# Cached-value rounds and gate quarters moved to other steps of the delta rule in a one-core hybrid decoder step

## The chip, the core and the metric

The program runs on one core of a Trainium2 chip. TensorE (PE) multiplies, VectorE (DVE) and ScalarE (ACT) read its results out of PSUM, GpSimd (POOL) helps with elementwise work, and SyncE (SP) issues most of the transfers. The metric is the device time of one execution in microseconds (us), the median of the runs.

## What is computed

One decoder layer for a prompt of 512 tokens and for 8 sample tokens with cached keys and values of 2048 positions each. One projection of the normalised input feeds two mixers and two gates; cut to what matters here:

```python
qkv, z, b_lg, a_lg, qb, kb, vb, ga, gb = in_proj(hp, norm1_w, w_in)     # ga, gb: 2 x 1024 gate columns
# A: gated delta rule, chunk by chunk (here chunks of 128 tokens, 4 chunks)
t_inv = triangular_solve(a + eye, eye)                                  # per chunk and head
v_new = ui - wi @ state
o = (qi * exp(gi)) @ state + qki @ v_new
state = state * exp(g_last) + k'^T @ v_new
y_a = (rmsnorm(o) * silu(z)) @ w_proj_a
# B, sample tokens: attention over the cached pages chosen by q . mean(k)
o = softmax(logits) @ cached values
y_b = o @ w_proj_b
mixed = sigmoid(ga) * y_a + sigmoid(gb) * y_b
```

After it come the output projection, the MLP and a final norm. The outputs are the activations, the new keys and values, and the new states.

## The kernel before

All matmuls are float32. A large one is split in three (high x high, high x low, low x high), in `product` at L463. A "unit" is 128 output columns of a weight for all 520 tokens: ScalarE makes the high half of the weights (`split_high`, L447), VectorE the low half (`split_low`, L452). The 16 gate units, two sets of 8, are each cut into quarters of 12 matmuls; `gate(n, first, last)` issues them, and a unit's last quarter is followed on ScalarE by its tanh (L1037), then by the high half for the unit two further on.

The order is written out by hand. `delta_order()` lists 92 steps: the stages of the delta rule for chunk 0, then 2 (slot 0) interleaved with those of chunk 1, then 3 (slot 1), four stages behind. `delta_fill()` hangs other work on each step by its number: gate quarters, low halves (`low`), rounds of cached values (`round`), the mask after each fourth round (`mask`). Each engine walks the same list, does its part of the stage, then its part of the step's fills, `low` first.

The stages of a chunk: sums, decays, turn, products, start; then left and right of levels 1 to 6 of the triangular inverse (left: four transposes L2222 and small products L2168 or L2228, each copied out by ScalarE; right: small products L2168 or L2239, taken over by VectorE with a mask, L1620, or a copy, L1622); inverse_k, new_v, new_state (products for the state, then for the output o, all L2155); normalise (ScalarE squares o at L1111, VectorE reduces it, ScalarE takes the root at L1114); turn_out (VectorE scales by the root's reciprocal, L1585 and L1586, and PE turns the result, L2175); keep_out.

A **round** (`value_round`, L2146) multiplies weights of one sample token with four pages of cached values, in two halves of two pages. The pages lie in `ring`, which holds four halves: so pages of a round are asked for only once the round two before it has been done. SP issues these loads (L601). Each sample token takes 4 rounds, 32 in all; the first round of a token also waits until VectorE has read the last token's result out of the bank (`keep_values`, L1573 and L1576). In the version before, rounds 0 to 25 and gate units 1 to 8 are hung on the steps, and units 9 to 15 come behind the last step with rounds 26 to 31 between whole units.

The lines of the delta loop that place this work on PE:

```python
for what, k in filled[i]:
    if what == "gate":
        gate(k // 4, 2 * (k % 4), 2 * (k % 4) + 2)
    ...
    elif what == "round":
        value_round(k)
```

Of the kernel before, what the change touches and what calls it, by code (L numbers as in the profile page):

```python
# [26 lines left out]
ALU = mybir.AluOpType  # L27
ACT = mybir.ActivationFunctionType
# [6 lines left out]
P = 128  # L35
# [87 lines left out]


KEYS_BEFORE = sum(keys_in_unit(u) for u in range(U_C)) + sum(keys_in_step(n) for n in range(NA))
ROUNDS_DELTA = 26
GATES_DELTA = 9


def delta_fill():  # L130

    fill = [[] for _ in range(len(delta_order()))]
    for i in range(GROUPS - KEYS_BEFORE):
        fill[i - (i >= 9)].append(("key", i))
    quarters = [0, 1, 1, 2, 2, 3, 3, 6, 8, 9, 10, 11, 13, 14, 16, 17, 18, 19, 20, 21, 36, 42, 43, 45, 46, 47, 48, 82, 83, 88, 89]
    for i, at in enumerate(quarters):
        fill[at].append(("gate", 5 + i))
    for name, at in (("sm_prep", 2), ("sm_bcast", 4), ("sm_bc", 4), ("sm_turn", 8), ("sm_delta", 9), ("sm_osq", 10), ("sm_osum", 12),
                     ("sm_oms", 13), ("sel_turn", 15), ("sel_red", 16), ("sel2_turn", 17), ("select", 18), ("bias", 20),
                     ("lg_bias", 21), ("lg_exp", 21), ("row_sums", 22), ("den", 25), ("den_out", 26), ("sm_oroot", 36), ("sm_on", 39),  # L140
                     ("sm_oh", 40), ("sm_onl", 41)):
        fill[at].append((name, 0))
    for u, at in ((3, 3), (4, 6), (5, 14), (6, 19), (7, 30), (8, 47), (9, 60)):
        fill[at].insert(0, ("low", u))
    for half in range(2):
        fill[5 + half].append(("sm_kv", half))
        fill[6 + half].append(("sm_rows", half))
    for k in range(3):
        fill[11 + k].append(("tail", k))
        fill[12 + k].append(("tail_out", k))  # L150
    for r in range(ROUNDS_DELTA):
        at = 24 + 13 * r // 5 + (r == 24)
        fill[at].append(("round", r))
        if r % 4 == 3:
            fill[at + 1].append(("mask", r // 4))
            if r == 15:
                fill[at + 2].append(("turn_values", 0))
    return fill
# [43 lines left out]
def hybrid_step(nc, const_f, const_m, x_prompt, x_sample, cache_k, cache_v, page_table, state_delta, state_conv,  # L202
# [9 lines left out]
    with ExitStack() as ctx:  # L212
# [123 lines left out]
        sts7 = at("sts7", [P, HA, DA], F32, ht_at + 3 * NT * 4)  # L336
        sqc = at("sqc", [P, 2 * HA, DA], F32, d0 + 16384)
        gate_b = at("gate_b", [P, 8, NT], F32, d0)
        mh = at("mh", [P, KT, NT], F32R, r1)
        ml = at("ml", [P, KT, NT], F32R, r1 + 16640)  # L340
        sga = at("sga", [P, NT], F32, r1 + 53248)
# [14 lines left out]
        def unit_ps(b):  # L356

            return ps[:, b * 1024 + 256:b * 1024 + 256 + NT]
# [130 lines left out]
            return unit_ps(u % 2 if u else 3)  # L489

        def gate_ps(n):
            return unit_ps(0 if 0 < n < GATES_DELTA else 1 if n == 0 else n % 2)

        def slot_banks(p):

# [322 lines left out]
        def _(act):  # L818
# [210 lines left out]
            def gate(n):  # L1029

                u = U_GATE + n
                if n < 12:
                    load_unit(act, u + 4)
                act.wait_ge(unit_done, u + 1)
                if n == 3:
                    act.wait_ge(*done("sm_kv1"))
                A((gate_a if n < 8 else gate_b)[:, n % 8], gate_ps(n), ACT.Tanh, scale=0.5).then_inc(S["gate_out"], 1)  # L1037
                split_high(act, u + 2)

            gate(0)  # L1040
# [109 lines left out]
            act.wait_ge(S["s_out"], NCH)  # L1150
            act.dma_start(sd_prompt[0, 0].rearrange("h d e -> d h e"), st[:, NCH % 2]).then_inc(stored, 16)
            act.wait_ge(S["ona_l_out"], NCH)
            for n in range(9, 15):
                gate(n)
            act.wait_ge(*done("os_ready"))
            A(onb_h[:, :, SEQ:NT], s4[:, 0:32].rearrange("p (c b) -> p c b", c=4), ACT.Copy).then_inc(*did("os_h"))
# [67 lines left out]
        def _(v):  # L1224
# [364 lines left out]
            for i, (stage, c) in enumerate(delta_order()):  # L1589
# [89 lines left out]
                        keep_values(n)  # L1679
                if i == 0:  # L1680
                    split_low(v, U_GATE + 2)
            split_low(v, U_GATE + 10)
            split_low(v, U_GATE + 11)
            keep_values(6)
            for u in range(U_GATE + 12, U_GATE + 17):
                split_low(v, u)
            keep_values(7)
            v.wait_ge(S["vb_turned"], 2)
# [19 lines left out]
            for j in range(8):  # L1708
                u = U_MERGE + j
                v.wait_ge(unit_done, u + 1)  # L1710
                v.wait_ge(S["gate_out"], 16)
                b = 2 * (1 - j % 2)
                link(STT(sga[:], gate_a[:, j], 1.0, unit_ps(b), ALU.add, ALU.mult))
                link(STT(sgb[:], gate_b[:, j], 1.0, unit_ps(b + 1), ALU.add, ALU.mult))
                if j >= 1:
                    v.wait_ge(S["mh_out"], j)
                TT(mx_[:], sga[:], sgb[:], ALU.add).then_inc(S["mix_ready"], 1)
                if j < 7:
                    split_low(v, u + 2)
                v.wait_ge(S["mix_ready"], j + 1)  # L1720
                v.wait_ge(S["mh_out"], j + 1)
                STT(ml[:, j], mx_[:], 0.5, mh[:, j].bitcast(F32), ALU.mult, ALU.subtract).then_inc(S["ml_out"], 1)
                v.wait_ge(S["ml_out"], j + 1)
# [86 lines left out]
        def _(pe):  # L1810
# [478 lines left out]


            pe.wait_ge(S["on_gated"], NCH - 1)
            gate(9)
            value_round(26)
            gate(10)
            value_round(27)
            gate(11)
            value_round(28)
            gate(12)
            value_round(29)
            gate(13)  # L2300
            value_round(30)
            gate(14)
            value_round(31)
            gate(15, 0, 4)
            turn_values(1)
# [108 lines left out]
```

## Time and profile before

| | before |
|---|---|
| median of 3 runs (lowest to highest) | 967.5 us (966.75 to 967.82) |
| the profiled execution: its time | 968.5 us |
| its span, first to last instruction | 966.0 us |
| PE busy | 936.7 us, 97% |
| DVE, ACT, POOL busy | 516.3, 400.9, 231.4 us |
| mean granted TensorE clock | 0.992 of 2.4 GHz |
| first round to last round | 329.3 to 483.9 us |

The profiled execution took 2.5 us more than its span, and 1.0 us more than the median of the runs. PE is busy nearly throughout, so what can change is where PE stands idle, and busy time of a merged row in which PE waited between matmuls.

### The profile page before, as it was taken

What the parts mean: (1) busy time and instruction counts of PE and PEld (TensorE: products, weight loads), DVE (VectorE), ACT (ScalarE), POOL (GpSimd) and SP (SyncE); (2) the same over time, 40 slices, a digit from 0 to 9 for tenths busy, and PEclk for the clock granted to TensorE, in tenths of its full rate; (3) what the DMA queues carried; (4) which work ended last, traced back from release to release, by engine and by line L of the source; (5) the groups of instructions that cost most, each with busy time, mean ns of one, the idle gap of its engine ahead of it and who ended that gap; (6) DMA issues with size and microseconds to landing.
All of it is one profiled execution on the core that took longest, in us unless ns stands there. A gap on an engine that the chain in (4) does not pass through costs nothing.

```text
span 966.0 us, 21253 instructions
## 1 busy us (share of the span) xinstructions
PE 936.7 (97%) x8658; PEld 879.7 (91%) x8658; DVE 516.3 (53%) x718; ACT 400.9 (41%) x695; POOL 231.4 (24%) x137
## 2 busy tenths in 40 slices
PE   5999999999997999999999999999999999999997
PEld 5999999999986776568899999999999999999997
DVE  6227598887886633433156556753344344334444
ACT  7435555556753345323122343521352144224433
POOL 0005975667779003000000002661000000000000
PEclk8999999999998999999999999999999999999999
DMA  8546696776686387877724852323322233344312
GB/s 252 171 169 220 211 304 194 216 217 194 187 270 209 96 255 239 278 238 239 219 69 125 271 152 87 89 88 98 100 88 88 88 92 101 89 139 122 89 41 88
DMA packets 184173, 156.50 MB, mean 162 GB/s; under 512 B 9217, under 2 KB 146123, under 8 KB 183702
## 3 DMA queue, kind: packets, MB, share of 16 engines
q1 hardware_dynamic: 165126, 141.33, 48.0%
q10 hardware_dynamic: 18968, 14.07, 4.8%
q8 instruction: 56, 0.92, 0.4%
q14 instruction: 23, 0.19, 0.1%
HBM read 146.51 MB, written 8.95 MB: 161 GB/s over the span
## 4 chain that ended last, share of the span: by engine, by line
PE 84%; POOL 4%; DVE 4%; issue 3%; DMA 2%; ACT 1%; SPq 1%; DVEq 0%; ACTq 0%; POOLq 0%
PE ps L463 69%; PE ps L2146 3%; POOL ring L769 3%; PE ps L2155 3%; PE ps L1998 2%; PE ps L1816 1%; DMA ring<-in_cache_v 1%; PE ps L1965 1%; PE ps L2168 1%; PE ps L1855 1%; PE ps L1988 1%; PE ps L2175 1%; DVE w_low L452 1%; DMA w_raw<-in_w_in 1%; PE ps L2222 1%
## 5 line engine op out<-in xcount | busy, mean ns | idle before, releaser
L463 PE MATMUL ps<-xh,w_high 128*128 128x256 f32 x1216 | 256.4, 292 | 1.4 <-DVE w_low L452 0.9
L463 PE MATMUL ps<-xl,w_high 128*128 128x256 f32 x1216 | 245.3, 283 | 0.0
L463 PE MATMUL ps<-xh,w_low 128*128 128x256 f32 x1216 | 245.3, 283 | 0.0
L452 DVE TENSOR_TENSOR w_low<-w_raw,w_high 128x1024 fp32r<-128x1024 f32 x125 | 163.8, 1311 | 150.9 <-ACT w_high L447 150.6
L447 ACT ACTIVATE w_high<-w_raw 128x1024 fp32r<-128x1024 f32 x125 | 132.2, 1058 | 262.3 <-PE ps L463 258.7
L463 PEld LDWEIGHTS ps<-xh,w_high 128*128 128x128 f32 x1216 | 187.8, 189 | 16.3 <-issue 11.4
L463 PEld LDWEIGHTS ps<-xh,w_low 128*128 128x128 f32 x1216 | 189.1, 189 | 0.0
L463 PEld LDWEIGHTS ps<-xl,w_high 128*128 128x128 f32 x1216 | 188.9, 189 | 0.0
L769 POOL TENSOR_TENSOR ring<-ring,qb 128x1024 f32<-128x1024 f32 x64 | 152.9, 2411 | 130.9 <-DVE mtqk L1287 74.4
L463 PE MATMUL ps<-ml,w_high 128*128 128x256 f32 (+1 forms) x640 | 128.9, 283 | 0.0
L463 PE MATMUL ps<-mh,w_low 128*128 128x256 f32 (+1 forms) x640 | 128.9, 283 | 0.0
L463 PE MATMUL ps<-mh,w_high 128*128 128x256 f32 (+1 forms) x640 | 128.5, 282 | 0.0
L463 PEld LDWEIGHTS ps<-ml,w_high 128*128 128x128 f32 x640 | 99.2, 188 | 0.0
L463 PEld LDWEIGHTS ps<-mh,w_low 128*128 128x128 f32 x640 | 99.2, 188 | 0.0
L463 PEld LDWEIGHTS ps<-mh,w_high 128*128 128x128 f32 x640 | 99.2, 188 | 0.0
L1272 DVE TENSOR_REDUCE lg<-ring 128x16 f32<-128x1024 f32 x64 | 77.3, 1214 | 17.2 <-POOL ring L769 17.1
L1763 DVE TENSOR_TENSOR ht<-ps,ht 128x520 f32<-128x520 f32 x31 | 21.7, 700 | 90.8 <-PE ps L463 90.8
L809 POOL TENSOR_TENSOR state<-state,sbc 128x512 f32<-128x512 f32 x8 | 10.9, 1367 | 227.3 <-PE ps L463 227.3
L2146 PE MATMUL ps<-ring,lg 128*32 128x512 f32 x256 | 42.2, 619 | 0.7 <-DMA ring<-in_cache_v 0.6
L1181 ACT ACTIVATE mh<-uu 128x520 fp32r<-128x520 f32 x32 | 20.5, 639 | 38.2 <-DVE uu L1768 38.2
L1752 DVE TENSOR_TENSOR ml<-uu,mh 128x520 fp32r<-128x520 f32 x32 | 22.4, 701 | 24.8 <-ACT mh L1181 24.8
L953 ACT ACTIVATE prob<-ps,nbias 128x128 f32<-128x128 f32 (+3 forms) x32 | 16.8, 525 | 28.0 <-DVE nbias L1385 28.0
(375 smaller groups left out, 1116.8 us busy)
## 6 DMA issues: line engine op xcount, KB each, us to landing
ring<-in_cache_k SPq DMA_DIRECT2D x128, 256.0 KB, 3.3
ring<-in_cache_v SPq DMA_DIRECT2D x128, 256.0 KB, 3.5
w_raw<-in_w_in SPq DMA_DIRECT2D x66, 256.0 KB, 3.9
w_raw<-in_w_up SPq DMA_DIRECT2D x64, 256.0 KB, 3.1
w_raw<-in_w_down SPq DMA_DIRECT2D x64, 256.0 KB, 3.0
w_raw<-in_w_in ACTq DMA_DIRECT2D x24, 256.0 KB, 4.2
w_raw<-in_w_out SPq DMA_DIRECT2D x16, 256.0 KB, 3.2
ht_dram<-ht ACTq DMA_DIRECT2D x1, 2080.0 KB, 15.3
```

Of the source, the lines that this page charges most:

```text
L447: act.activation(w_high[:, u % 2], w_raw[:, s], ACT.Copy).then_inc(S_hi, 1)
L452: dve.tensor_tensor(w_low[:, u % 2], w_raw[:, u % 4], w_high[:, u % 2].bitcast(F32), ALU.subtract).then_inc(S_lo, 1)
L463: last = pe.matmul(out[:, a:b], w[:, u % 2, k, :], x[:, i, a:b], start=(first + i == 0 and w is w_high and x is rhs_h), stop=(first + i == ...
L769: g.tensor_tensor(ring[:, r % 4], ring[:, r % 4], bc(qb[:, b:b + 1, :], [P, 2, WB]), ALU.mult)\
L953: A(prob[:, n % 2, 0:N], score_bank(n, N), ACT.Exp, scale=-1.0, bias=nbias[:, n % 3:n % 3 + 1], accum_out=rs[:, n:n + 1]).then_inc(S["att_ ...
L1181: A(mh[:, i - 1], uu[:, (i - 1) % 2], ACT.Copy).then_inc(S["uh_out"], 1)
L1272: v.tensor_reduce(lg[:, b, :, 2 * r:2 * r + 2].rearrange("p h g -> p g h"), ring[:, i % 4].rearrange("p g (h d) -> p g h d", d=DB), AX.X, ...
L1752: TT(ml[:, i - 1], uu[:, (i - 1) % 2], mh[:, i - 1].bitcast(F32), ALU.subtract)\
L1763: TT(ht[:, j], unit_ps((U_MLP + i) % 2), ht[:, j], ALU.add).then_inc(S["h_out"], 1)
L1998: last = mm(rows_bank[:, h * DB:(h + 1) * DB], probt[:, n % 2, t * P:(t + 1) * P], mtv[:, t, h * DB:(h + 1) * DB], start=(t == 0), stop=(t ...
L2146: last = mm(bank(6)[32 * strip:32 * strip + 32, :], lg[:, b].rearrange("p h (s r) -> p r (h s)", r=4)[:, part], ring[:, g % 4, i, :], star ...
L2155: last = mm(out[:, h * P:(h + 1) * P], left(h), right(h), start=(i == 0), stop=(i == len(pairs) - 1), skip_group_check=True)
```

## The change

It replaces the formula that spaced the rounds by a list of steps, hangs 24 rounds in place of 26 on the steps, and leaves eight for the end, where they stand between parts of the last gate units. The quarters of gate units 6 to 8 move to other steps, and unit 9 joins them, in ten-unit numbering (`GATES_DELTA = 10`). So that gate units 8 and 9 can be kept while the delta rule still uses its buffers, their results go to a new place, `gate_89`, in memory that the chunks 0 and 1 of `tm` have left. The low halves 7 to 10 move with them.

```diff
-ROUNDS_DELTA = 26
-GATES_DELTA = 9
+ROUND_ITEMS = (24, 27, 29, 31, 33, 38, 40, 42, 45, 48, 50, 54, 56, 58, 62, 66, 69, 72, 75, 78, 80, 81, 84, 87)
+GATES_DELTA = 10
...
-    for r in range(ROUNDS_DELTA):
-        at = 24 + 13 * r // 5 + (r == 24)
+    for r, at in enumerate(ROUND_ITEMS):
...
+        gate_89 = at("gate_89", [P, 2, NT], F32, r1 + 33280)
...
-            return unit_ps(0 if 0 < n < GATES_DELTA else 1 if n == 0 else n % 2)
+            return unit_ps(0 if 0 < n < GATES_DELTA else 1 if n == 0 else (n + 1) % 2)
...
-                A((gate_a if n < 8 else gate_b)[:, n % 8], gate_ps(n), ACT.Tanh, scale=0.5).then_inc(S["gate_out"], 1)
+                A(kept_gate(n), gate_ps(n), ACT.Tanh, scale=0.5).then_inc(S["gate_out"], 1)
...
-            gate(9)
+            value_round(24)
+            gate(10, 0, 6)
+            value_round(25)
+            gate(10, 6, 8)
+            gate(11, 0, 4)
             value_round(26)
-            gate(10)
+            gate(11, 4, 8)
+            gate(12, 0, 2)
             value_round(27)
-            gate(11)
+            gate(12, 2, 8)
             value_round(28)
-            gate(12)
+            gate(13, 0, 4)
             value_round(29)
-            gate(13)
+            gate(13, 4, 8)
+            gate(14, 0, 2)
             value_round(30)
-            gate(14)
+            gate(14, 2, 8)
             value_round(31)
```

Behind the step at which gate unit 5 ends, the quarters of units 6 to 8 stood at steps 21, 36, 42, 43, 45, 46, 47, 48, 82, 83, 88 and 89, and stand at 21, 28, 30, 32, 39, 41, 47, 50, 55, 58, 62 and 68; unit 9 has 72, 75, 81 and 84. The low halves 7, 8, 9 stood at 30, 47, 60 and stand at 29, 43, 57; the tenth is new at 74.

Below, numbers behind names (`sqb_128`) are buffers; line numbers from L1037 on are 3 higher in the changed kernel.

**The end of the delta rule, PE.** L2155 (L2158) is new_state of chunk 3, L463 a gate unit, L2175 (L2178) the transposes of turn_out of chunk 3, L2146 (L2149) a round. Before:

```order
L2155 MATMUL ps<-st,qgt 128x128
L2155 MATMUL ps<-An,qkt 128x128
L2155 MATMUL ps<-st,qgt 128x128
L2155 MATMUL ps<-An,qkt 128x128
L463 MATMUL ps<-xh,w_high 128x256
L463 MATMUL ps<-xh,w_high 128x264
```

Of the change:

```order
L2158 MATMUL ps<-An,qkt 128x128
L2158 MATMUL ps<-st,qgt 128x128
L2158 MATMUL ps<-An,qkt 128x128
L2178 MATMUL ps<-cf,sqb_128 128x128 x4
L2149 MATMUL ps<-ring,lg 32x512 x4
L463 MATMUL ps<-xh,w_high 128x256
```

Two gate quarters and a round stood between new_state and turn_out of chunk 3; now nothing does. ScalarE at the same place, from the copies of chunk 2's last products on (L1114 or L1117 the root, L1037 or L1040 the tanh of a gate). Before:

```order
L1103 ACTIVATE Dm<-ps 128x512
L1119 ACTIVATE ona_h<-An 128x4x128
L1106 ACTIVATE An<-ps 128x512
L1111 ACTIVATE sqb_128<-ps 128x512
L1114 ACTIVATE on_st<-on_st 128x4
L437 DMA w_raw<-in_w_in 128x4x128 x2
L1037 ACT_TABLE_LOAD
```

Of the change:

```order
L1040 ACT_TABLE_LOAD
L1040 ACTIVATE gate_154<-ps 128x520
L447 ACTIVATE w_high<-w_raw 128x1024
L1106 ACTIVATE Dm<-ps 128x512
L1122 ACTIVATE ona_h<-An 128x4x128
L1109 ACTIVATE An<-ps 128x512
L1114 ACTIVATE sqb_128<-ps 128x512
L1117 ACT_TABLE_LOAD
L1117 ACTIVATE on_st<-on_st 128x4
```

A tanh of gate unit 9 now stands ahead, so the root of chunk 3 has a table load of its own; over the program ScalarE has two rows more, both of them such loads.

**The first turn_out, PE.** From the output products of chunk 0 (L2155, L2158) over left and right of level 6 of chunk 1 to turn_out of chunk 0 (L2175, L2178). Before, with the first two rows of a gate quarter's twelve:

```order
L2155 MATMUL ps<-An,qkt 128x128 x4
L2146 MATMUL ps<-ring,lg 32x512 x4
L2222 MATMUL ps<-cf,Em 64x64 x4
L2228 MATMUL ps<-Em,An 64x64 x4
L463 MATMUL ps<-xh,w_high 128x256
L463 MATMUL ps<-xh,w_high 128x264
```

Of the change:

```order
L2158 MATMUL ps<-An,qkt 128x128 x4
L2225 MATMUL ps<-cf,Em 64x64 x4
L2231 MATMUL ps<-Em,An 64x64 x4
L2242 MATMUL ps<-sqb_128,Dm 64x64 x4
L2178 MATMUL ps<-cf,sqb_127 128x128 x4
L2149 MATMUL ps<-ring,lg 32x512 x4
```

Two rounds and a quarter have gone from between the output products and turn_out.

**The mask at step 43, VectorE.** L1632 (L1635) is the state of chunk 1, L1576 (L1579) the mask that round 8 waits for, L452 a low half. Before:

```order
L1486 TENSOR_TENSOR ona_l<-sn,ona_h 128x4x8
L1632 SCALAR_TENSOR_TENSOR st<-st,glx,ps 128x128 x4
L1576 SCALAR_TENSOR_TENSOR vb<-ps,cf,vb 128x512
L1598 TENSOR_TENSOR sqb_127<-tm,egc 128x512
L1637 TENSOR_REDUCE on_st<-sqb_128 128x4
```

Of the change:

```order
L1489 TENSOR_TENSOR ona_l<-sn,ona_h 128x4x8
L1635 SCALAR_TENSOR_TENSOR st<-st,glx,ps 128x128 x4
L452 TENSOR_TENSOR w_low<-w_raw,w_high 128x1024
L1579 SCALAR_TENSOR_TENSOR vb<-ps,cf,vb 128x512
L1601 TENSOR_TENSOR sqb_127<-tm,egc 128x512
```

The low half of gate unit 8 has moved ahead of the mask.

## Rows read from the trace of the kernel before

**Rows 1.** The page, busy us (share of the span) and instructions by engine

```profile
PE 936.7 (97%) x8658; PEld 879.7 (91%) x8658; DVE 516.3 (53%) x718; ACT 400.9 (41%) x695; POOL 231.4 (24%) x137
```

**Rows 2.** Windows: us, PE, PEld, DVE, ACT, POOL busy, clock, DMA share, GB/s

```profile
295.00:300.00 5.00, 1.89 (x42) 1.22 (x42) 4.79 (x15) 1.25 (x3) 5.00 (x3) 0.94 0.71 231
300.00:305.00 5.00, 3.33 (x16) 3.34 (x17) 5.00 (x5) 1.67 (x3) 5.00 (x4) 0.50 0.42 127
```

**Rows 3.** Tile view of the value ring, 326 to 490 us

```profile
L2146 PE MATMUL ps<-ring,lg x256: 592/619/650, 329.3 to 483.9; 128*32 128x512 f32 x128
...
  DMA ring<-in_cache_v: 6.8, 11
...
DMA to landing us min/median/max: 2.6/3.5/6.2
```

**Rows 4.** Timeline of PE: start us, us, line, tiles; four rounds

```profile
335.83 1.95 PE L2146 MATMUL ps<-ring,lg 128*32 128x512 f32 x8
...
405.70 2.23 PE L2146 MATMUL ps<-ring,lg 128*32 128x512 f32 x8
...
410.17 2.12 PE L2146 MATMUL ps<-ring,lg 128*32 128x512 f32 x8
...
414.49 1.10 PE L2146 MATMUL ps<-ring,lg 128*32 128x512 f32 x8
```

**Rows 5.** Waits of PE, 329 to 500 us: total us, times, longest

```profile
PE ps L2168 <- ACT qgt L1088: 0.7, 1, 0.7
PE ps L2168 <- ACT sqb L1098: 0.6, 2, 0.4
...
PE ps L2222 <- DVE Em L1620: 0.6, 1, 0.6
PE ps L2175 <- ACT An L1055: 0.5, 1, 0.5
...
PE ps L2175 <- DVE Dm L1611: 0.2, 1, 0.2
```

**Rows 6.** Timelines of PE, ACT and DVE up to turn_out of chunk 0

```profile
347.31 0.50 PE L463 MATMUL ps<-xh,w_high 128*128 128x256 f32 x2
...
348.94 0.68 PE L2239 MATMUL ps<-sqb,Dm 64*64 64x64 f32 x8
...
347.41 0.38 ACT L1100 ACTIVATE sqb<-ps 64x256 f32<-64x256 f32 x1 [0.23 <-PE ps L2228]
347.81 1.28 ACT L1114 ACT_TABLE_LOAD   x1
...
349.55 0.69 DVE L1586 TENSOR_TENSOR sqb<-ps,on_st 128x512 f32<-128x512 f32 x1
```

**Rows 7.** Timelines of PE, ACT and DVE up to turn_out of chunk 3

```profile
438.02 0.48 PE L463 MATMUL ps<-xh,w_high 128*128 128x256 f32 x2
...
442.11 0.66 PE L2175 MATMUL ps<-cf,sqb 128*128 128x128 f32 x4
...
438.30 0.60 ACT L1111 ACTIVATE sqb<-ps 128x512 f32<-128x512 f32 x1 [3.31 <-PE ps L2155]
439.86 0.20 ACT L1114 ACTIVATE on_st<-on_st 128x4 f32<-128x4 f32 x1 [0.96 <-DVE on_st L1638]
...
440.31 0.69 DVE L1586 TENSOR_TENSOR sqb<-ps,on_st 128x512 f32<-128x512 f32 x1
```

**Rows 8.** Timelines of DVE and PE around the state of chunk 1

```profile
336.61 1.21 DVE L452 TENSOR_TENSOR w_low<-w_raw,w_high 128x1024 fp32r<-128x1024 f32 x1
...
360.37 1.12 DVE L1632 SCALAR_TENSOR_TENSOR st<-st,glx,ps 128x128 f32<-128x128 f32 x4 [5.23 <-PE ps L2155]
361.41 0.74 DVE L1576 SCALAR_TENSOR_TENSOR vb<-ps,cf,vb 128x512 f32<-128x512 f32 x1
...
361.88 0.49 PE L463 MATMUL ps<-xh,w_high 128*128 128x256 f32 x2
```

**Rows 9.** Timeline of ACT, the high half behind a gate's tanh

```profile
376.22 1.05 ACT L447 ACTIVATE w_high<-w_raw 128x1024 fp32r<-128x1024 f32 x1
```

More of the change, by code:

```diff
@@ L134, in delta_fill @@
         fill[i - (i >= 9)].append(("key", i))
-    quarters = [0, 1, 1, 2, 2, 3, 3, 6, 8, 9, 10, 11, 13, 14, 16, 17, 18, 19, 20, 21, 36, 42, 43, 45, 46, 47, 48, 82, 83, 88, 89]
+    quarters = [0, 1, 1, 2, 2, 3, 3, 6, 8, 9, 10, 11, 13, 14, 16, 17, 18, 19, 20, 21, 28, 30, 32, 39, 41, 47, 50, 55, 58, 62, 68, 72, 75, 81, 84]
     for i, at in enumerate(quarters):
@@ L142, in delta_fill @@
         fill[at].append((name, 0))
-    for u, at in ((3, 3), (4, 6), (5, 14), (6, 19), (7, 30), (8, 47), (9, 60)):
+    for u, at in ((3, 3), (4, 6), (5, 14), (6, 19), (7, 29), (8, 43), (9, 57), (10, 74)):
         fill[at].insert(0, ("low", u))
@@ L491, in gate_ps, with kept_gate @@
         def gate_ps(n):
-            return unit_ps(0 if 0 < n < GATES_DELTA else 1 if n == 0 else n % 2)
+            return unit_ps(0 if 0 < n < GATES_DELTA else 1 if n == 0 else (n + 1) % 2)
+        def kept_gate(n):
+            return gate_a[:, n] if n < 8 else gate_89[:, n - 8] if n < 10 else gate_b[:, n - 8]
         def slot_banks(p):
@@ L1152, in _ @@
             act.wait_ge(S["ona_l_out"], NCH)
-            for n in range(9, 15):
+            for n in range(10, 15):
                 gate(n)
@@ L1681, in _ @@
                     split_low(v, U_GATE + 2)
-            split_low(v, U_GATE + 10)
             split_low(v, U_GATE + 11)
+            split_low(v, U_GATE + 12)
             keep_values(6)
-            for u in range(U_GATE + 12, U_GATE + 17):
+            for u in range(U_GATE + 13, U_GATE + 17):
                 split_low(v, u)
@@ L1713, in _ @@
                 link(STT(sga[:], gate_a[:, j], 1.0, unit_ps(b), ALU.add, ALU.mult))
-                link(STT(sgb[:], gate_b[:, j], 1.0, unit_ps(b + 1), ALU.add, ALU.mult))
+                link(STT(sgb[:], kept_gate(8 + j), 1.0, unit_ps(b + 1), ALU.add, ALU.mult))
                 if j >= 1:
```

## The prediction

> **What bounds the kernel now.** First the page: PE is busy 97% of the span, no other engine much over half [rows 1]. So a change of order can only give or take time in which PE stands still, or in which a merged row of PE holds waits between its matmuls. The number of matmuls, halves, rounds and transfers is the same in both kernels, and nothing ahead of step 24 moves; I therefore look from the first round at 329.3 us on [rows 3].
>
> Second, the view of the ring: PE stood idle 6.8 us in 11 waits for pages of cached values, and a page took 2.6 to 6.2 us from its issue to its landing, median 3.5 [rows 3]. The timeline shows what such a wait costs a round. A round that finds all pages takes 1.10 us, as at 414.49; those at 335.83, 405.70 and 410.17 take 1.95, 2.23 and 2.12 [rows 4]. Ten rounds between 335.83 and 410.17 are longer than 1.10. Their excess, with 0.4 us that PE waited ahead of one of them, sums to 7.8 us. That is 1.0 more than the idle rows say, because a second half that comes late no longer overlaps the first. So 7.8 us is the most that better spacing can give.
>
> Third, the other waits of PE in this stretch: 0.7, 0.6 (two together), 0.6, 0.5 and 0.2 us, each for a copy by ScalarE or VectorE that the next product of the delta rule needs [rows 5]. They are small because gate quarters and rounds stand between a product and the one that needs it. This is the cover that the change moves.
>
> **The ring: gained.** Pages of a round are asked for when the round two before is done. In the trace the rounds that waited began 6.2 to 8.3 us after the round two before; the one at 414.49, 8.8 us after that at 405.70, did not wait [rows 4]. I added up PE's work between rounds in the new order, with each item's size from the trace (round 1.1, gate quarter 1.5 to 1.6, a left step 0.4 to 1.0, a right step 0.4 to 0.6, new_state 2 to 2.8). With the new waits below, a round now begins 7.3 to 12.9 us after the round two before; only rounds 2, 11, 12, 21 and 22 are at 8.3 or less. If these five lose a quarter of a us each, 1.2 us stays, against 0.8 for each of the ten before. Bounds: nothing stays, or 3 us does. Gain 7.8 - 1.2 = **6.6 us**, between 4.8 and 7.8.
>
> **The last turn_out (chunk 3): lost.** Before, PE's next work behind the output products began at 438.02, two gate quarters and a round, and turn_out followed at 442.11. Meanwhile ScalarE squared the output (438.30), took the root (439.86) and VectorE scaled it until 440.31 + 0.69 = 441.00 [rows 7]. So PE needed 441.00 - 438.02 = 3.0 us of other work and had 4.1. In the new order nothing stands there. The tanh of unit 9 is now ahead, so a table load of 1.28 us [rows 6] comes between square and root: 438.90 + 1.28 = 440.18 in place of 439.86, 0.3 more. PE stands still **3.3 us**, between 3.0 and 3.4.
>
> **The first turn_out (chunk 0): lost.** Two rounds and a quarter leave this place. In the trace the products of level 6 ended at 347.31, and ScalarE's copy of them at 347.41 + 0.38 = 347.79; the right step needs that copy, so without the quarter PE waits 0.5 us [rows 6]. From the copy on, table load, root, reciprocal and scaling took until 349.55 + 0.69 = 350.24, which is 2.45 us; PE has only the right step to do, 0.6 us of its row's 0.68 before the next can start [rows 6]. That leaves 1.85 us, in all **2.3 us**. Least 1.5, if ScalarE gets to the copy earlier; most 2.6.
>
> **Round 8: lost.** It starts the third token's bank and so waits for the mask, and at step 43 the low half of unit 8 now stands ahead of it on VectorE. From 361.41 the low half takes 1.21 (as at 336.61) and the mask 0.74, less 0.1 of overlap: 363.3 us. PE's output products ended at 361.88, and round 8 comes next where a quarter used to be [rows 8]. **1.4 us**, between 1.2 and 1.6. Behind the low half and the mask stand VectorE's reduction and scaling for turn_out of chunk 1; PE has a round and a turn for cover, 2.1 us, against six short operations of 2.6 us in sum: **0.4 us**, between 0 and 1.0.
>
> **Steps 50 to 54: lost.** Between products and start of chunk 2 stood a gate quarter, and PE still waited 0.2 us [rows 5]: the chain takes 1.8 us. Now a round of 1.1 stands there: **0.6 us** more. The tanh of unit 7 moves from step 48 to 50, behind the copies of start: the waits of 0.7 and 0.5 us for qgt and An [rows 5] go, but its table load, 0.6 us of tanh and 1.05 us of high half [rows 9] now stand ahead of the copy of left1. PE has a round, sums and left1 meanwhile. I take **0.9 us**, between 0 and 1.3.
>
> **Pairs of small steps: lost and gained.** Three places now have a left or right step directly ahead of the one that needs its copy, with only a small step between: right3 of chunk 2 (step 62), left6 (72) and right4 of chunk 3 (75). The rows of this kind are 0.4 and 0.6 us [rows 5]; I take 0.5 each, **1.5 us**, between 0.9 and 2.0. In return the three such waits of the kernel before (0.6 in two, 0.6) are covered, which with qgt and An makes 2.4 us gained.
>
> **At no cost.** The place of `gate_89`, the other PSUM bank of the last units and the seam between rounds and gate parts at the end: rounds there already stood among gates unhurt, and none of the last eight waited for pages. Two table loads more on ScalarE are 2.6 us of an engine that is 41% busy [rows 1]; one is in the 3.3 us above, the other lies under a gate's matmuls, and would cost its 1.28 us if that cover were gone. VectorE reads each mask in time for rounds 4, 12, 16, 20, 24 and 28, with at least 0.5 us to spare by the same durations.
>
> **The sum.** New waits 3.3 + 2.3 + 1.4 + 0.4 + 0.6 + 0.9 + 1.5 = 10.4; gone 2.4; ring gained 6.6. Net 10.4 - 2.4 - 6.6 = **1.4 us longer**. On the profiled execution that is 968.5 + 1.4 = 969.9 us; this one stood 1.0 over the median of its runs, so the median should be 967.5 + 1.4 = **968.9 us**. With the gains and losses at their ends the net runs from -3 to +5 us.
>
> **A rule on the table loads.** In the rows the load at 347.81 takes 1.28 us, and root and reciprocal are over when the scaling starts 1.74 us later [rows 6]; load, root and reciprocal alone come to 1.7, so nothing else stands between. The Trainium skill, page "ScalarE: Activation LUTs", section "What ACT_TABLE_LOAD costs", gives about 2.66 us for each switch of set, the load and a drain of 1.38 us behind it. By that the new load ahead of the last root would cost PE an estimated 1.4 us more, and the sum would be 2.8 us longer instead of 1.4. The trace leaves no room for the drain, so my sum goes by the trace.
>
> **Rivals.**
> 1. Faster: ScalarE and VectorE run ahead more than I think, because PE no longer bunches rounds. Then only the wait at the last turn_out has full size, which has nothing to stand under, and the six others shrink to the 0.5 us of the small rows [rows 5], 3.0 in all. Net 6.3 - 2.4 - 6.6 = -2.7: 964.8 us. It decides once the new waits together are under 7.1 us. For it: before, nine in ten of these steps had no wait. Against it: the chains are counted from starts and ends in the trace, and the order has nothing to put under them. Chance 0.22.
> 2. Slower, the clock: around 295 to 305 us PE was busy 1.89 and 3.33 of 5 us and the granted clock fell to 0.94 and 0.50 of 2.4 GHz [rows 2], that is to 1.2 GHz for a while, 0.3 + 2.5 = 2.8 us of full clock lost. If the stillness at the first or last turn_out does the same, 1.4 + 2.8 = 4.2: 971.7 us. Against it: there PE stood still for over half of the first stretch, here it works fully up to the last turn_out and again behind it. The Trainium skill, page "TensorE: Matmul & The Clock Gate", section "What's actually happening", has a monitor that halves the clock after idleness and restores it after steady work; the trace agrees in kind. Chance 0.1.
> 3. Slower, the spacing doesn't do it: landing takes up to 6.2 us [rows 3] and loads of units 12 and 13 now fall among the pages. If half of the 7.8 us stays, the net is 10.4 - 2.4 - 3.9 = 4.1: 971.6 us. It decides from a remainder of 1.7 us on. Chance 0.15.
> 4. Slower with the same waits, each near its upper end, 970 to 971 us: chance 0.11.
>
> **How the numbers follow.** About 0.2%, 1.9 us, is what a measurement of this kernel can tell from no change. The forecast, within 1.9 us of 967.5, has 0.42; rival 1 gives faster 0.22; rivals 2 to 4 give slower 0.36. The range reaches to rival 1's value and a little past those of 2 and 3: 964.8 to 972.3 us.
>
> **What would show it.** Right: the ring's idle under 2 us and no round over 1.9; PE idle over 3 us ahead of the last turn_out and some 2 ahead of the first, 1.4 ahead of the ninth round, for VectorE's mask. Wrong: turn_out of chunk 3 starting under 2.5 us after the last output product, a clock under 1.00 anywhere from 350 us on, or waits for `in_cache_v` over 3 us.

## The result: slower than forecast, by lost clock

| kernel | executions | median us | lowest to highest | ratio to before, 95% interval |
| --- | --- | --- | --- | --- |
| before | 4 | 967.66 | 966.75 to 968.65 | |
| changed | 4 | 974.38 | 970.16 to 977.35 | 1.0066 [1.0041, 1.0090] |
| changed, taken again (e1) | 6 | 974.79 | 972.87 to 979.61 | 1.0076 [1.0052, 1.0100] |

The forecast was 968.9 us with a range to 972.3. The kernel is 6.7 us slower. Its four executions spread over 7 us where the four of the kernel before lay within 2; the later sets of the kernel before, 19 to 22 executions each, spread over 5 to 7 us as well. One execution of the kernel before, in the set beside e9 and e10, took 4782.69 us; it is in that set's median of 968.16 us, and in no ratio, interval or mean.

The execution that was profiled is the fastest of the changed kernel, 970.16 us with a span of 967.8 us; that of before had 966.0 us. The page and PE's waits, to be read beside [rows 1] and [rows 5]:

```profile
span 967.8 us, 21255 instructions
PE 933.4 (96%) x8658; PEld 878.0 (91%) x8658; DVE 518.7 (54%) x718; ACT 403.3 (42%) x697; POOL 231.5 (24%) x137
...
PE ps L2178 <- DVE sqb L1589: 5.6, 3, 3.1
PE ps L2171 <- ACT sqb L1101: 2.0, 4, 1.0
PE ps L2149 <- DVE vb L1579: 1.2, 1, 1.2
PE ps L2158 <- ACT Dm L1106: 0.7, 1, 0.7
PE ps L2178 <- DVE Dm L1614: 0.6, 1, 0.6
PE ps L2242 <- ACT sqb L1103: 0.5, 1, 0.5
PE ps L2225 <- DVE Em L1623: 0.4, 1, 0.4
PE ps L2149 <- DMA ring<-in_cache_v: 0.4, 1, 0.4
```

Each row is who waited for whom, total us, times, longest. The first row is turn_out of chunks 3, 0 and 1. From 325 to 500 us all rows but the ring's, with one of 0.2 us that is not shown, make 11.2 us; in the same stretch of the kernel before they made 4.0.

The ring's own view, beside [rows 3]: idle before its loads and matmuls, and landing.

```profile
  DMA ring<-in_cache_v: 1.8, 2
...
DMA to landing us min/median/max: 2.4/3.3/5.6
```

The idle on pages fell from 6.8 us in 11 waits to 1.8 in 2. This view adds up the idle of weight loads and of matmuls (6.2 in 9 and 0.6 in 2 before, 1.3 and 0.4 now), so the two that are left are one late page, of round 22. Now PE around the two places with the longest waits (start us, us, line, tiles, idle before and its releaser), which are those of [rows 6] and [rows 7]:

```profile
347.07 0.68 PE L2242 MATMUL ps<-sqb,Dm 64*64 64x64 f32 x8 [0.47 <-ACT sqb L1103]
349.52 0.66 PE L2178 MATMUL ps<-cf,sqb 128*128 128x128 f32 x4 [1.78 <-DVE sqb L1589]
350.11 1.57 PE L2149 MATMUL ps<-ring,lg 128*32 128x512 f32 x8
...
445.64 0.66 PE L2178 MATMUL ps<-cf,sqb 128*128 128x128 f32 x4 [3.15 <-DVE sqb L1589]
446.23 1.94 PE L2149 MATMUL ps<-ring,lg 128*32 128x512 f32 x8
...
448.70 0.64 PE L463 MATMUL ps<-xl,w_high 128*128 128x256 f32 x2
...
449.83 0.40 PE L463 MATMUL ps<-xl,w_high 128*128 128x256 f32 x2
```

The waits are those forecast. What was not forecast stands in the rows behind them: the round after each takes 1.57 and 1.94 us where a full round takes 1.10, and no page was late for it. A pair of gate matmuls takes 0.64 us and, a microsecond later, 0.40. The windows (us; PE, PEld, DVE, ACT, POOL busy; granted clock; DMA share; GB/s) say why:

```profile
345.00:350.00 5.00, 2.75 (x30) 2.21 (x29) 2.75 (x7) 2.84 (x6) 0.00 (x0) 1.00 0.85 301
350.00:355.00 5.00, 5.00 (x29) 3.61 (x28) 1.67 (x8) 1.26 (x3) 0.00 (x0) 0.66 0.43 121
440.00:445.00 5.00, 2.50 (x23) 2.31 (x21) 2.92 (x9) 2.08 (x3) 0.00 (x0) 1.00 0.62 210
445.00:450.00 5.00, 4.36 (x22) 2.54 (x23) 3.54 (x7) 0.73 (x2) 0.00 (x0) 0.66 0.25 69
```

PE stands still for 2.3 us in two waits (0.47 and 1.78, with 0.68 of small matmuls between) and for 3.2 us in one. Right behind each, the granted clock averages 0.66 of 2.4 GHz over five microseconds. A mean of 0.66 is 3.4 us at 1.2 GHz and the rest at 2.4, and costs 0.34 x 5 = 1.7 us, twice. In the execution profiled in e1 the second is twice as long, this time over two windows:

```profile
445.00:450.00 5.00, 2.56 (x23) 2.37 (x22) 2.86 (x9) 2.08 (x3) 0.00 (x0) 0.98 0.65 210
450.00:455.00 5.00, 4.29 (x18) 2.31 (x19) 3.10 (x7) 0.63 (x1) 0.00 (x0) 0.50 0.20 56
455.00:460.00 5.00, 5.00 (x40) 4.56 (x38) 0.51 (x1) 1.28 (x1) 0.00 (x0) 0.83 0.96 295
```

There (0.02 + 0.50 + 0.17) x 5 = 3.4 us of clock go, the first part of it while PE still waits.

### The profile page after: what moved, and what is told of

Read it like the earlier page. It is cut to its first block, busy times and chain, and to the rows that moved or that the text cites. A ratio compares the mean times of both kernels' runs of the same rounds, so it can differ in the third digit from the quotient of the medians.

```text
span 967.8 us, 21255 instructions
## 1 busy us (share of the span) xinstructions
PE 933.4 (96%) x8658; PEld 878.0 (91%) x8658; DVE 518.7 (54%) x718; ACT 403.3 (42%) x697; POOL 231.5 (24%) x137
## 4 chain that ended last, share of the span: by engine, by line
PE 87%; DVE 5%; ACT 3%; DMA 1%; POOL 1%; issue 1%; SPq 0%; DVEq 0%; ACTq 0%
PE ps L463 71%; PE ps L2149 3%; PE ps L2158 2%; PE ps L2001 2%; PE ps L1819 2%; PE ps L2171 1%; POOL ring L772 1%; PE ps L1968 1%; DVE w_low L452 1%; PE ps L1991 1%; PE ps L2225 1%; DVE lg L1275 1%; PE ps L1858 1%; DMA ring<-in_cache_v 1%; PE ps L2178 0%
## 5 line engine op out<-in xcount | busy, mean ns | idle before, releaser
L463 PE MATMUL ps<-xh,w_high 128*128 128x256 f32 x1216 | 257.2, 293 | 1.4 <-DVE w_low L452 1.0
L463 PE MATMUL ps<-xl,w_high 128*128 128x256 f32 x1216 | 245.2, 283 | 0.0
L463 PE MATMUL ps<-xh,w_low 128*128 128x256 f32 x1216 | 245.0, 283 | 0.0
L452 DVE TENSOR_TENSOR w_low<-w_raw,w_high 128x1024 fp32r<-128x1024 f32 x125 | 163.4, 1308 | 148.8 <-ACT w_high L447 148.5
L463 PEld LDWEIGHTS ps<-xh,w_high 128*128 128x128 f32 x1216 | 187.8, 189 | 17.4 <-issue 12.3
L463 PEld LDWEIGHTS ps<-xl,w_high 128*128 128x128 f32 x1216 | 188.8, 188 | 0.0
L463 PEld LDWEIGHTS ps<-xh,w_low 128*128 128x128 f32 x1216 | 188.8, 189 | 0.0
L463 PE MATMUL ps<-ml,w_high 128*128 128x256 f32 (+1 forms) x640 | 128.9, 283 | 0.0
L463 PE MATMUL ps<-mh,w_low 128*128 128x256 f32 (+1 forms) x640 | 128.9, 283 | 0.0
L463 PE MATMUL ps<-mh,w_high 128*128 128x256 f32 (+1 forms) x640 | 128.5, 282 | 0.0
L463 PEld LDWEIGHTS ps<-ml,w_high 128*128 128x128 f32 x640 | 99.2, 188 | 0.0
L463 PEld LDWEIGHTS ps<-mh,w_low 128*128 128x128 f32 x640 | 99.2, 188 | 0.0
L463 PEld LDWEIGHTS ps<-mh,w_high 128*128 128x128 f32 x640 | 99.2, 188 | 0.0
L2149 PE MATMUL ps<-ring,lg 128*32 128x512 f32 x256 | 37.4, 641 | 1.7 <-DVE vb L1579 1.2
L1623 DVE COPY_PREDICATED Em<-cm,ps 128x512 f32<-128x512 uint8 x20 | 14.6, 734 | 30.6 <-PE ps L2171 30.6
```

Source lines behind the costliest of these rows:

```text
L452: dve.tensor_tensor(w_low[:, u % 2], w_raw[:, u % 4], w_high[:, u % 2].bitcast(F32), ALU.subtract).then_inc(S_lo, 1)
L463: last = pe.matmul(out[:, a:b], w[:, u % 2, k, :], x[:, i, a:b], start=(first + i == 0 and w is w_high and x is rhs_h), stop=(first + i == ...
L2149: last = mm(bank(6)[32 * strip:32 * strip + 32, :], lg[:, b].rearrange("p h (s r) -> p r (h s)", r=4)[:, part], ring[:, g % 4, i, :], star ...
```

## Work and clock, told apart

Every execution lists its span and its mean granted clock. Span times clock is about the span at full clock; span less that product is what lower clock took (a low clock while PE waits anyway is counted too, so this is an upper value). As each clock is given to three digits, a single product is good to half a microsecond; these are means over the executions.

| kernel | executions | median us | mean span | mean clock | product | lost to clock |
| --- | --- | --- | --- | --- | --- | --- |
| before | 22 | 967.57 | 965.0 | 0.9923 | 957.5 | 7.5 |
| changed, both sets | 10 | 974.4, 974.8 | 972.3 | 0.9870 | 959.6 | 12.7 |
| e2, stand-ins at both turn_outs | 8 | 971.39 | 968.9 | 0.9918 | 960.9 | 8.0 |
| e3, last turn_out covered | 12 | 965.97 | 964.0 | 0.9908 | 955.1 | 8.9 |
| e4, all large waits covered | 6 | 959.74 | 957.5 | 0.9918 | 949.6 | 7.9 |
| e5, low half 8 behind the mask | 6 | 972.75 | 970.4 | 0.9883 | 959.0 | 11.4 |
| e6, new rounds alone | 7 | 973.64 | 971.0 | 0.9890 | 960.4 | 10.6 |
| e7, new gates alone | 12 | 970.00 | 967.1 | 0.9907 | 958.1 | 9.0 |
| e8, before with a bare last turn_out | 10 | 973.32 | 970.2 | 0.9907 | 961.1 | 9.1 |
| e9, e8 with stand-ins | 10 | 972.11 | 969.4 | 0.9916 | 961.2 | 8.2 |
| e10, stand-ins at the last turn_out | 12 | 971.52 | 969.3 | 0.9912 | 960.8 | 8.5 |

The row of before is the set beside e5 to e8; the set beside e1 to e4 gives the same product, 967.45 us and 8.0 lost to clock, the set beside e9 and e10 a product of 957.4, 968.16 us (967.88 without the execution of 4782.69) and 8.5. So the last column moves by 1 us from set to set with the kernel unchanged. The change costs 2.1 us of work, which is near the 1.4 of the sum, and 5.2 us of clock.

The clock also falls where the change does not reach. From 15 to 20 us, before and of the change:

```profile
15.00:20.00 5.00, 2.24 (x10) 2.27 (x11) 3.94 (x10) 3.72 (x10) 0.00 (x0) 0.60 0.95 221
15.00:20.00 5.00, 2.15 (x18) 2.18 (x19) 3.95 (x10) 3.72 (x10) 0.00 (x0) 1.00 0.97 222
```

PE works and stands still about alike in both, and one execution lost clock there while the other did not. Up to 325 us, where all these kernels are alike, the windows of the profiles add up to between 3.4 and 8.5 us of lost clock (before 6.8, changed 3.4, e1 8.5). So the clock or the time of one execution says little about one place: the windows at that place do, and means over executions. The experiments ask whether that clock is lost because of the waits at the turn_outs.

## Experiments

**e1: the changed kernel again.** No edit.

> The changed kernel once more, to see how its time and its granted clock go together. Clock theory (the waits cost 1 to 2 us as such, and the rest of the loss is TensorE at 1.2 GHz behind the longest waits): the time again near 974 us, its executions 4 us or more apart, and span less the time lost to the clock the same in all, 959 to 960 us. Work theory (the new order costs more PE time by itself, the clock has no part): executions within 1 us of each other around 974 us, at the clock of the kernel before.

974.79 us. The slower executions are those with the lower clock: 979.61 us at 0.983, 972.87 at 0.988. The products lie between 958.8 and 960.8. So the spread of this kernel is one of clock, at the turn_outs and elsewhere.

**e2: something to do under the waits.** Stand-ins are matmuls of the 128x128 identity by itself into a bank that nobody reads at that time; they are work that the reference does not have.

```diff
+STAND_IN = {37: 2, 38: 7, 90: 13}
+                if i in STAND_IN:
+                    pe.wait_ge(S["gate_out"], 7 if i < 40 else 10)
+                    stand_in(STAND_IN[i])
```

> The changed kernel with 22 small matmuls that compute nothing used, set into the three waits of PE for ScalarE and VectorE: 2 ahead of right6 of chunk 1, 7 ahead of turn_out of chunk 0, 13 ahead of turn_out of chunk 3. They are shorter than the waits, so the waits as such stay. Clock theory: the clock stays at full speed at both places (two stretches of 3.4 us at 1.2 GHz go, 1.7 us each), and the median falls by 3 to 5 us to 969 to 971 us. Work theory: no change from the changed kernel, within 0.5 us.

971.39 us, 1.0033 [1.0016, 1.0050], a little over the 969 to 971 that the clock theory gave; the intervals of e1 and e2 do not meet. The timeline and the windows of e2:

```profile
445.82 2.84 PE L2185 MATMUL ps<-cf 128*128 128x128 f32 x24
448.90 0.66 PE L2179 MATMUL ps<-cf,sqb 128*128 128x128 f32 x4 [0.24 <-DVE sqb L1590]
449.49 1.10 PE L2150 MATMUL ps<-ring,lg 128*32 128x512 f32 x8
...
350.00:355.00 5.00, 5.00 (x49) 4.21 (x51) 2.68 (x9) 2.84 (x6) 0.00 (x0) 1.00 0.81 291
445.00:450.00 5.00, 4.76 (x45) 4.10 (x44) 2.92 (x8) 2.09 (x3) 0.00 (x0) 1.00 0.51 157
```

The copies that turn_out needs came no sooner: stand-ins of 2.84 us and 0.24 idle fill the same gap. Yet the clock behind stays at 1.00 in both places, and the round takes 1.10 us again. 3.4 us came back although PE did more. This shows that the missing clock was bound to the stillness and not to the order of the work.

**e3: cover for the last turn_out.** The last three gate quarters of unit 9 and the last four rounds of the steps move to steps where PE would stand still.

```diff
-ROUND_ITEMS = (..., 78, 80, 81, 84, 87)
+ROUND_ITEMS = (..., 78, 81, 86, 87, 88)
-    quarters = [..., 68, 72, 75, 81, 84]
+    quarters = [..., 68, 72, 83, 88, 89]
```

> The changed kernel with its last turn_out covered again: the last three quarters of unit 9 at steps 83, 88, 89, the last four rounds at 81, 86, 87, 88. Clock theory: the 3.3 us wait goes, 0.9 us at new_v of chunk 3 and the 1.7 us of lost clock behind it too: 5 to 6 us less than the changed kernel, 968 to 969.5 us. Work theory: 3.3 us less. If PE's waits don't bound it there, no change.

965.97 us, 0.9986 [0.9974, 0.9998], 8.8 us under e1 and better than either expectation. The row for `sqb` at L1589 falls from 5.6 us to 2.4 in two waits, and the last turn_out is the row without idle:

```profile
442.73 0.66 PE L2178 MATMUL ps<-cf,sqb 128*128 128x128 f32 x4
443.31 1.10 PE L2149 MATMUL ps<-ring,lg 128*32 128x512 f32 x8
...
445.00:450.00 5.00, 5.00 (x42) 4.05 (x42) 1.83 (x2) 0.21 (x1) 0.00 (x0) 1.00 0.94 301
```

By the table 4.5 us are work and 3.8 clock. The rows show 3.15 us of this wait gone, 0.7 of the one for `Dm` at new_v of chunk 3, and the 1.5 us of the late page: no round takes over 1.13 us now. The first turn_out's wait and the dip behind it are still there (clock 0.89 from 350 to 355 us and 0.77 in the five behind, again 1.7 us).

**e4: cover everywhere.** New places for rounds, quarters and low halves, chosen so that each chain found above has PE work beside it.

```diff
+ROUND_ITEMS = (24, 28, 31, 34, 36, 40, 42, 44, 46, 49, 51, 55, 57, 60, 65, 68, 69, 74, 78, 80, 82, 86, 87, 88)
+    quarters = [..., 20, 21, 32, 37, 37, 46, 49, 53, 53, 58, 62, 66, 66, 82, 83, 88, 89]
+    (7, 29), (8, 53), (9, 74), (10, 88)
```

> The changed kernel with all 24 rounds, the quarters of units 6 to 9 and the low halves 8 to 10 placed so that, by the durations of the traces, every wait in the stretch has work under it and rounds still begin over 7 us after the round two before. Sum of the waits removed against the changed kernel: 3.3 + 2.3 + 1.2 + 0.6 + 0.6 + 1.0 + 1.6 = 10.6 us, and 3.4 us of lost clock. Clock theory: 958 to 963 us, under the kernel before by 5 to 9 us. Rival (the ring sets the pace once the waits go): waits for pages of 3 to 7 us come in their place, 963 to 968 us.

959.74 us, 0.9922 [0.9907, 0.9937]: 7.7 us under the kernel before, 15 under the changed one. PE's waits from 320 to 500 us are these and no more:

```profile
PE ps L2158 <- ACT Em L1083: 1.0, 1, 1.0
PE ps L2171 <- ACT sqb L1101: 0.5, 1, 0.5
PE ps L2134 <- DVE vb L1582: 0.2, 1, 0.2
```

Three rounds take 1.6, 1.6 and 2.0 us, for late pages inside them, 1.9 us too long in sum where the kernel before has 7.4 inside its rounds. So nearly even spacing of the rounds and covered turn_outs are no rivals. The change under study had the first and gave up the second.

**e5: one term of the sum, round 8 behind the mask.**

```diff
-    for u, at in (..., (8, 43), ...):
+    for u, at in (..., (8, 45), ...):
```

> The changed kernel with one number altered: the low half of unit 8 stands at step 45, behind the mask of rounds 4 to 7, in place of step 43. In the trace of the changed kernel PE waits 1.2 us for that mask ahead of round 8; the wait should go down to at most 0.2 us, and the row of PE's waits for vb at L1579 with it. Sum-of-waits theory: 1.2 us shorter than the changed kernel, about 973.4 us, with the dips of the clock at the two turn_outs as before. Clock theory: the same 1.2 us and nothing more, since no dip stood behind this wait in either trace of the changed kernel. Rival, that the waits move rather than go: the reduction for turn_out of chunk 1 waits no longer, but PE's next wait for the low half (gate unit 8's first quarter) takes its place, and the time stays at 974.6.

972.75 us, 1.0056 [1.0038, 1.0074], whose interval meets e1's, so the time alone decides nothing. The rows do. The row of the mask at L1579 is gone, but turn_out of chunk 1 behind it waits longer, 1.47 us where it waited 0.64:

```profile
366.17 1.10 PE L2149 MATMUL ps<-ring,lg 128*32 128x512 f32 x8
...
369.76 0.66 PE L2178 MATMUL ps<-cf,sqb 128*128 128x128 f32 x4 [1.47 <-DVE sqb L1589]
```

1.2 us gone and 0.8 come back. The rival that waits move was right in kind, and named the wrong place.

**e6: the rounds' places without the gates'.** The kernel before with the new `ROUND_ITEMS`, eight rounds among the last gates; unit 9 and the quarters as before. The low half of unit 12 moves ahead of one `keep_values`, which is not shown below.

```diff
+ROUND_ITEMS = (24, 27, 29, ..., 81, 84, 87)
+            for n in range(9, 14):
+                value_round(n + 15)
+                gate(n)
+            value_round(29)
+            gate(14, 0, 4)
+            value_round(30)
+            gate(14, 4, 8)
```

> The kernel before with the new places of the rounds alone (24 of them in the steps, 8 among the last gates); unit 9 and the gate quarters stay where they were. My own adding up of durations, which gives the kernel before 7.4 us of waits on the ring, gives 8.3 here: the new places even out PE's work only together with the quarters' new places. Other waits grow by 1.3 us. The last turn_out keeps two quarters as cover and no round: a wait of about 1 us or none. Sum of waits: 2.3 us over the kernel before, 969.8 us. If instead the rounds' places alone carry the gain on the ring, the ring's row falls under 3 us and the time to 963 to 965. Clock: no wait over 2 us near a turn_out, so no new dip; if the clock does fall at a turn_out, the time is 1.7 to 3.4 us more.

973.64 us, 1.0060 [1.0036, 1.0084]. The ring stays bad, as expected: in its view

```profile
  DMA ring<-in_cache_v: 6.1, 7
```

and the product is 2.9 us over before (2.3 expected). On the clock I was wrong. There is no wait over 1.0 us in the stretch, and the clock falls all the same, for longer than anywhere else:

```profile
400.00:402.50 2.50, 2.14 (x56) 1.43 (x52) 1.26 (x3) 0.54 (x1) 0.00 (x0) 1.00 0.87 252
402.50:405.00 2.50, 1.51 (x14) 1.31 (x12) 0.94 (x2) 0.65 (x2) 0.00 (x0) 1.00 0.83 281
405.00:407.50 2.50, 2.50 (x52) 1.16 (x52) 0.00 (x0) 1.09 (x2) 0.00 (x0) 0.67 0.29 106
407.50:410.00 2.50, 2.25 (x51) 1.83 (x50) 1.33 (x2) 0.38 (x1) 0.00 (x0) 0.50 0.65 204
```

It is back at 1.00 from 420 us on; 6.8 us are lost here in this execution. The mean over the seven executions is 3.1 us of clock over that of before, so they hardly all lost as much. Ahead of it PE had idled 0.36 and 0.99 us among the small products of the left and right steps. The same small products stood at 400 to 412 us in the kernel before, with waits for pages in their rounds, and at full clock. Why this execution crossed over there and stayed low for some 14 us no run here settles.

**e7: the gates' places without the rounds'.** The changed kernel with the old formula for 26 rounds and six rounds among the last gates.

```diff
-ROUND_ITEMS = (24, 27, 29, ..., 81, 84, 87)
+ROUND_ITEMS = tuple(24 + 13 * r // 5 + (r == 24) for r in range(26))
```

> The changed kernel with the rounds put back to the old formula (26 in the steps, 6 among the last gates); unit 9 and the quarters stay spread. The same adding up gives a ring of 0.6 us (if so, the quarters' spread is what cured the ring, not the rounds' places), and waits of 2.0 us at the last turn_out, which has a round again as cover, about 1 us at the first, 1.8 at start of chunk 2 and 1.4 at round 8. Sum of waits: 1.3 us over the kernel before, 968.8 us. Clock theory: with both turn_outs' stillness a third to a half shorter, the dips behind them come in some executions or not at all; 968.8 with none, 970.5 to 972 with one or two.

970.00 us, 1.0023 [1.0006, 1.0040]. That lies between the 968.8 expected without a dip and the 970.5 to 972 with one or two. The idle on the ring is 0.2 us in one wait. With e6 this shows that what cured the ring is the spread of the quarters; by the order of the steps it puts a quarter of 1.5 us between rounds that had followed closely. The rounds' new places did next to nothing for it alone (6.1 us against 6.8). The last turn_out has a round as cover again:

```profile
446.30 0.66 PE L2178 MATMUL ps<-cf,sqb 128*128 128x128 f32 x4 [2.12 <-DVE sqb L1589]
...
440.00:445.00 5.00, 4.19 (x36) 2.97 (x32) 1.98 (x6) 1.78 (x2) 0.00 (x0) 1.00 0.62 174
445.00:450.00 5.00, 3.70 (x31) 3.70 (x32) 3.17 (x8) 0.93 (x3) 0.00 (x0) 1.00 0.91 277
```

2.1 us of stillness and no dip in this execution, against 3.15 us and a dip in every profile that has it without stand-ins (changed, e1, e5). This execution, 967.6 us, is one of the faster; those of up to 973.43 us, at a clock of 0.988, have no profile.

**e8: the bare turn_out in the kernel before.** Everything as before, but the two quarters at steps 88 and 89 stand behind turn_out, and round 25 at step 87.

```diff
-    quarters = [..., 82, 83, 88, 89]
+    quarters = [..., 82, 83, 90, 91]
-        at = 24 + 13 * r // 5 + (r == 24)
+        at = 24 + 13 * r // 5 + (r == 24) - 2 * (r == 25)
```

> The mirror image of e3: the kernel before with only the cover of the last turn_out taken away, everything else alike. Two gate quarters (steps 88 and 89) move behind turn_out and round 25 moves from step 89 to 87, which leaves the matmuls, halves, tanhs and transfers the same. PE then needs the 3.0 us that the chain from the output products to the scaled values took in the trace of before, and has nothing. Sum of waits: PE stands still 3.0 us, 967.5 + 3.0 = 970.5 us at the same clock as before. Clock theory: the same wait, and behind it a stretch at 1.2 GHz of 3.4 or 6.8 us, which costs 1.7 to 3.4 more: 972.2 to 974, with a mean clock lower by 0.002 to 0.004. Against both: if something else of the chain ran later, under 969.

973.32 us, 1.0050 [1.0032, 1.0068], within what the clock theory gave. The idle is 2.79 us, by the table the work costs 3.6 us (round 25 also waits 0.6 for its page) and the clock 1.6:

```profile
443.13 0.87 PE L2175 MATMUL ps<-cf,sqb 128*128 128x128 f32 x4 [2.79 <-DVE sqb L1586]
...
440.00:445.00 5.00, 2.21 (x14) 2.02 (x13) 2.69 (x8) 0.80 (x2) 0.00 (x0) 0.84 0.80 278
445.00:450.00 5.00, 5.00 (x37) 5.00 (x36) 1.02 (x3) 3.47 (x4) 0.00 (x0) 0.82 0.55 145
```

The windows again show 1.7 us lost, (0.16 + 0.18) x 5. One uncovered chain, in a kernel that is otherwise the tuned one, is worth nearly as much as the whole change. Three of the ten executions are at 0.993 and 969.0 to 970.3 us, no more than the wait alone would give. Whether the dip was missing there or another one, ahead of the first round, no profile shows.

**e9 and e10: stand-ins at the last turn_out alone,** 11 of them in e8's order and 13 in the changed kernel.

```diff
+STAND_IN = {90: 11}
+                if i in STAND_IN:
+                    pe.wait_ge(S["on_gated"], 3)
+                    stand_in(STAND_IN[i])
```

> e8 (the kernel before with the last turn_out bare) plus 11 matmuls of the 128x128 identity by itself at that place, into a bank that nobody reads: about 2.5 us of PE work under a wait that stays 2.8 us. Nothing that the kernel computes moves. Clock theory: the wait as such still costs its 2.8 us, but no dip of the clock stands behind it, so 1.7 to 2.5 us under e8's 973.3: 970.8 to 971.6 us, mean clock as of before (0.992). Rival, the clock has no part in it (the cost of the bare place is the wait and something else, such as the quarters' new places): e8's 973.3 us or a little more.

> The changed kernel with stand-in matmuls at the last turn_out alone (13 of them under its wait of 3.1 us), none at the first. Clock theory: the dip at 446 to 450 us goes, the one at 350 to 354 stays; e2, which covered both, gained 3.4 us against the changed kernel, so about half of it here: 972.5 to 973.5 us, clock 0.988 to 0.990. If one of the two dips carries all of the loss, 971.4 (the last) or 974.8 (the first).

e9: 972.11 us, 1.0038 [1.0023, 1.0054]. That is over the 970.8 to 971.6 expected and under the rival's 973.3. The profile shows the clock at 1.00 from 435 to 450 us, the product is e8's within 0.1 us, and the mean clock goes from 0.9907 to 0.9916, while before's own mean in the same two sets goes down, from 0.9923 to 0.9912. In time e9 is 1.5 us less than e8 when each is held against its own runs of before (967.57, and 967.88 without the long one), but the two intervals overlap, so the time alone does not show it. e10: 971.52 us, 1.0035 [1.0023, 1.0046], clearly under e1 and level with e2. In its profile the dip at the first turn_out is still there and the one at the last is gone:

```profile
350.00:355.00 5.00, 3.22 (x17) 1.10 (x15) 2.94 (x10) 1.09 (x3) 0.00 (x0) 0.73 0.37 140
440.00:445.00 5.00, 5.00 (x44) 4.07 (x43) 1.78 (x5) 1.15 (x2) 0.00 (x0) 1.00 0.56 172
445.00:450.00 5.00, 4.76 (x40) 3.59 (x40) 2.85 (x8) 2.12 (x4) 0.00 (x0) 1.00 0.26 96
```

So by the means the last turn_out carries most of the loss, 12.7 - 8.5 = 4.2 us of clock, and the first 0.5 by e2's row; in time e10 comes out at the 971.4 expected if the last carries all, not at the 972.5 to 973.5 of halves. The profiles divide it otherwise: each of the five that has the first turn_out bare (changed, e1, e3, e5, e10) shows 1.7 us lost behind it, and the three with the last one bare 1.7, 3.4 and 1.7. The means of the same kernel differ by 1 us between sets, so the division between the two places stays open; that stand-ins at the last one alone bring 3.3 us back is shown.

## Why the prediction was wrong, step by step

**The ring.** Forecast: 7.8 us become 1.2. Measured: one round is late for a page, round 22, which runs from 432.17 until the next work starts at 434.70, 1.5 us more than without the wait. So 1.5 stay and 6.3 are gained, near the 6.6 forecast. Round 22 was on the list of five; that the other four lost nothing and it lost 1.5 makes part of the agreement luck, and with 2.5 us it broke the sign "no round over 1.9".

**The last turn_out.** 3.3 forecast, 3.15 measured. The chain ran as written down from [rows 7]: square at 442.54, table load of 1.28, root at 444.45, scaling at 444.90. The root starts 0.02 us after the load's 1.28 us are over. The drain of 1.38 us that the Trainium skill, page "ScalarE: Activation LUTs", section "What ACT_TABLE_LOAD costs", adds to each load is not there; with it the wait would have been an estimated 4.5 us.

**The first turn_out.** 2.3 forecast, 0.47 + 1.78 = 2.25 measured. **Round 8:** 1.4 and 1.22. **turn_out of chunk 1:** 0.4 and 0.64. **start of chunk 2:** 0.6 and 0.59. **right1 of chunk 2:** 0.9 and 0.96. **The three pairs:** 1.5, and 0.43 + 0.44 + 0.19 = 1.1. All waits besides the ring grew by 11.2 - 4.0 = 7.2 us, where 10.4 - 2.4 = 8.0 were forecast. (The 4.0 hold a wait of 0.7 us for `Dm` at new_v of chunk 3 that the forecast's list of other waits left out; it is 0.7 in both kernels.)

**The sum.** 7.2 - 6.3 = 0.9 us, against 1.4 forecast, 1.8 between the two profiled spans and 2.1 between the products; 0.9 of the 1.8 stand in no wait counted here. That the profiled spans come so near the forecast is luck: by their windows both executions lost 6.8 us to the clock ahead of the last gates, that of before all of it ahead of the first round of values, that of the changed kernel one half there and one half at the turn_outs.

**The step that failed** is the clock. The sum put it at nothing, and rival 2, which had it, was priced at 2.8 us for one dip and given one chance in ten, with the argument that "there PE stood still for over half of the first stretch, here it works fully up to the last turn_out and again behind it". [Rows 2] showed a fall behind 3.1 us of idle in five; the forecast itself had 3.3 us of idle at the last turn_out. These are the same size, so the argument should have gone the other way. In the changed kernel PE is busy 2.50 of the five microseconds from 440, and 0.66 follows; a clock under 1.00 behind 350 us was the prediction's own sign of being wrong. The Trainium skill, page "TensorE: Matmul & The Clock Gate", section "What's actually happening", has the clock halved when PE has been idle. The traces agree in kind, with 0.50 in [rows 2] and 0.66 here, though from 15 to 20 us about the same idle brought a fall in one execution and none in another.

The price was too small as well. [Rows 2] break off inside the dip; the next window of the kernel before is still at 0.88:

```profile
305.00:310.00 5.00, 5.00 (x95) 4.45 (x95) 1.89 (x3) 1.91 (x4) 4.92 (x5) 0.88 0.77 259
```

So that one dip cost (0.06 + 0.50 + 0.12) x 5 = 3.4 us and not 2.8, and the change brought two. Measured: 5.2 us of clock on average. With it the forecast of 968.9 would have been 974.1, where 974.4 was measured.

**The remedy** that would have been visible: a chain of 3.0 us at the end of the delta rule needs 3.0 us of PE work beside it, whatever else is moved. e3 moves three quarters and four rounds for that, and is 8.8 us better than the change; in that are 1.5 us of the late page and 0.7 of the wait for `Dm`, which went too.

## What to carry to other kernels

Where PE is nearly always busy, a wait can cost more than its length: an uncovered chain of 3 us has a stretch at 1.2 GHz behind it in all four profiles that have one without stand-ins (changed, e1, e5, e8), which cost another 1.7 us in three of them and 3.4 in one. On average over the executions it was 1.6 us (e8) and 4.2 (the changed kernel). So price a new wait of that size at up to twice its length or a little more, and spend the independent work on the longest chains first; small waits of 0.5 us spread over many steps are the cheaper kind, but e6 shows that they aren't safe. When a kernel's executions spread over several microseconds, multiply span by mean clock before comparing, over ten executions or so: it tells whether work or clock was moved, and how much clock the same kernel loses from set to set.

## What was not expected of the hardware

- The clock fell behind 2.3 to 3.2 us of stillness in the midst of a stream that is 96% busy. The low stretch cost 1.7 us in one execution and 3.4 in another, at the same place with the same wait (3.15 and 3.14 us).
- From 15 to 20 us, with about the same work and idle, it fell to a mean of 0.60 in one execution and stayed at 1.00 in another.
- It fell in e6 with no single wait over 1.0 us, and stayed low until 420 us, the longest stretch at 1.2 GHz in any profile here.
- Identity matmuls under a wait of 3.1 us kept the clock at 1.00 behind it and gave 3.3 us back (e1 to e10), though nothing reads what they compute.
